# Block-product projections beside attention: sums in place, first output weights in four buffers, and the probabilities turned one product later

## The chip, the cores and the metric

The kernel runs on one core of one Trainium2 chip. The metric is device time in microseconds (us), the median of three runs. Five engines work side by side, each through its own queue in order: TensorE (PE: matrix products; PEld is its weight load), VectorE (DVE), ScalarE (ACT), GpSimd (POOL) and SyncE (SP, which here only issues DMAs). They wait for one another through semaphores.

## The reference, cut to what matters

Three residual layers act on 512 tokens of width 2048, and a norm ends the program. Everything is float32. The change lies in the third layer:

```python
def odd_layer(x, norm_g, w_in, b_forget, w_out):
    hn = rmsnorm(x, norm_g)
    proj = hn @ w_in
    q, k, v, z, f_logit = jnp.split(proj, cuts, axis=-1)
    log_f = jax.nn.log_sigmoid((f_logit + b_forget).astype(jnp.float32))
    o = forgetting_attention(q.reshape(shp), k.reshape(shp), v.reshape(shp), log_f)
    o = o * jax.nn.silu(z)
    return x + o @ w_out
```

There are 16 heads of width 128. `forgetting_attention` is causal softmax attention whose logits get the difference of two running sums of `log_f`.

## The kernel before

**Split operands.** A float32 operand is held as two parts, a rounded upper part (`_hi`) and the rest (`_lo`), and each product is three matmuls: hi by hi, hi by lo, lo by hi. ScalarE rounds (Copy into `w_hi`, `act_hi`), GpSimd or VectorE subtracts (`w_lo`, `act_lo`). Activations lie transposed, 16 tiles (`kt`) of 128 features by 512 tokens. A weight tile has 128 output columns in two halves of 8 `kt`, each 512 KB. Half 0 comes into `raw[:, 0]`, half 1 into `raw[:, 1]`, and `w_hi`, `w_lo` have four slots. `cast` (line 761) rounds a half; `rest` (line 3341) on GpSimd subtracts it in two instructions of 128x512 and raises `split_done`.

**Into the third layer (the forget stage).** `norm_vector(2)` scales each of 16 tiles into one of four buffers `norm_in` (line 721), ScalarE rounds it (706), VectorE subtracts (728). `first_tensor` multiplies the tiles of the forget logits and of head 0's q, then come k, v and the gate of head 0 as plain products (`gemm`, lines 338 to 340), 48 matmuls each. `first_vector` (441, 444) finishes the first two outputs, and ScalarE evacuates them (2679, 2682). TensorE's product for v waits for the evacuation of q. `forget_vector` and `forget_scalar` work out the running sum of the forget gates (16 rows) and store it as `decays`.

**The block products (w7).** The heads 1 to 15 have their projections made while attention for the head before runs. A pair of 128-column tiles by all tokens is done with 7 instead of 8 half-size products (Strassen, in Winograd's form). Each product is 24 matmuls of 128x256 (lines 2036 to 2039). The activation sides are S1 to S4, sums of quarters of the normed activations. They are made once, in two parts q = 0, 1 of four `kt` each. Before the change `fold_whole` (line 1897) first adds `act_hi` and `act_lo` back together into buffers of `arena`, four instructions for each q. `fold_sums` (1903 to 1909) makes the four sums and the rest of S1 (1911), `fold_round` (1919) rounds S1, S2, S4 on ScalarE, and `fold_gpsimd` (1926) subtracts S2 and S4. The two q share buffers, so q = 1 waits for GpSimd's rest of q = 0. S3 goes over a part of `act_hi` and `act_lo` (1934, 1939) once the gate's product has read it. `w7_vector` makes the weight sides in place (T1 2103, T2 2107, T3 2109, T4 2113; rests 2119), `w7_cast` (2053) rounds, and `w7_gpsimd` (2130) subtracts five of the seven. The raw quarters "11", "12", "21", "22" come from SyncE (`fetch`, 1978).

**One unit** is attention of head u and two w7 pairs (0 and 1) for head u+1. TensorE's order in `unit` is: scores (2177, `s`), product 0 of pair 0, the turn of v (2154), products 1 to 3, transposes of the probabilities (2188, `tp`), products 4 to 6, probabilities by v (2196, `pv`), the seven products of pair 1. The transposes wait for VectorE's scaling of the probabilities (2352, `sc3`), and `pv` waits for the lower part of the turned probabilities (2356, `pl`), which follows ScalarE's rounding (2231, `pt`). Product 4 needs `x2`, product 2's evacuation (2069), which stands behind the exponentials (2226) in ScalarE's queue. There are 15 such units, and a last attention without w7 pairs.

**Out of attention.** The last attention has the third output projection's first two tiles beside it (`gemm_two`, 362 to 364). It starts when three halves of their weights are split. Their four halves come through the two `raw` buffers in order: half 0 and half 1 of the first tile, then of the second, each load waiting for GpSimd to be done with the half before it in that buffer. The heads' results, stored in `mixed`, are loaded back into `mix` in five parts (line 3320), 3.75 MB.

## Time and profile before

| what | value |
|---|---|
| median of 3 runs | 3012.54 us (3011.49 to 3013.39) |
| the profiled execution | 3011.28 us, its span 3009.4 us |
| TensorE busy | 2894.2 us, 96% of the span |
| VectorE, ScalarE, GpSimd busy | 1594.5, 1302.0, 1432.3 us |
| mean granted TensorE clock | 0.99 |

Each execution's own time is 1.9 us over its span. A busy TensorE leaves only its waits to win, as its instructions stay the same here; so the profile is read for where TensorE sits idle, for how long, and what it waits for. The trace puts each wait down to the instruction that ended it. The stages are found by line: 338 to 340 plain products, 2036 to 2039 block products, 362 to 364 the first two output tiles.

### The profile page before, as it was taken

What the parts mean: (1) busy time and instruction counts of PE and PEld (TensorE: products, weight loads), DVE (VectorE), ACT (ScalarE), POOL (GpSimd) and SP (SyncE); (2) the same over time, 40 slices, a digit from 0 to 9 for tenths busy, and PEclk for the clock granted to TensorE, in tenths of its full rate; (3) what the DMA queues carried; (4) which work ended last, traced back from release to release, by engine and by line L of the source; (5) the groups of instructions that cost most, each with busy time, mean ns of one, the idle gap of its engine ahead of it and who ended that gap; (6) DMA issues with size and microseconds to landing.
All of it is one profiled execution on the core that took longest, in us unless ns stands there. A gap on an engine that the chain in (4) does not pass through costs nothing.

```text
span 3009.4 us, 52820 instructions
## 1 busy us (share of the span) xinstructions
PE 2894.2 (96%) x20478; PEld 2433.6 (81%) x20478; DVE 1594.5 (53%) x2101; ACT 1302.0 (43%) x1777; POOL 1432.3 (48%) x1037
## 2 busy tenths in 40 slices
PE   8999999999999999999999999996999999999898
PEld 6777777777877887887787778875999999999787
DVE  7555565343444138777723352146777767777312
ACT  6433344255655233333335453234455454545422
POOL 1223332533245446666543334434666666666643
PEclk9999999999999999999999999998999999999999
DMA  5111111222123433222242234431223222222433
GB/s 216 57 59 58 58 58 58 94 74 82 58 84 109 147 115 112 91 93 92 101 137 91 84 112 133 146 106 64 95 98 103 100 100 102 94 94 98 147 124 117
DMA packets 98561, 298.17 MB, mean 99 GB/s; under 512 B 10608, under 2 KB 16880, under 8 KB 97408
## 3 DMA queue, kind: packets, MB, share of 16 engines
q1 hardware_dynamic: 71440, 246.12, 24.2%
q10 hardware_dynamic: 26992, 50.22, 4.9%
q8 instruction: 95, 1.56, 0.2%
q14 instruction: 34, 0.28, 0.0%
HBM read 273.45 MB, written 22.84 MB: 98 GB/s over the span
## 4 chain that ended last, share of the span: by engine, by line
PE 77%; DVE 10%; issue 6%; ACT 3%; POOL 2%; DMA 1%; DVEq 0%; ACTq 0%; POOLq 0%; SPq 0%
PE ps L338 8%; PE ps L340 8%; PE ps L339 8%; PE ps L2036 6%; PE ps L2039 6%; PE ps L2038 6%; PE ps L1028 4%; PE ps L1029 4%; PE ps L1030 4%; PE ps L1348 3%; PE ps L1350 2%; PE ps L1349 2%; POOL w_lo L3341 2%; DVE arena L3147 1%; PE ps L1413 1%
## 5 line engine op out<-in xcount | busy, mean ns | idle before, releaser
L3341 POOL TENSOR_TENSOR w_lo<-raw,w_hi 128x512 fp32r<-128x512 f32 x632 | 849.6, 1368 | 1243.4 <-ACT w_hi L761 1242.3
L338 PE MATMUL ps<-act_hi,w_hi 128*128 128x512 f32 x1232 | 485.9, 394 | 17.5 <-POOL w_lo L3341 12.5
L761 ACT ACTIVATE w_hi<-raw 128x1024 fp32r<-128x1024 f32 x320 | 337.4, 1055 | 361.9 <-PE ps L340 142.8
L340 PE MATMUL ps<-act_lo,w_hi 128*128 128x512 f32 x1232 | 480.4, 390 | 0.0
L339 PE MATMUL ps<-act_hi,w_lo 128*128 128x512 f32 x1232 | 480.1, 390 | 0.0
L2130 POOL TENSOR_TENSOR w_lo<-raw,w_hi 128x512 fp32r<-128x512 f32 x150 | 233.8, 1579 | 151.1 <-ACT w_hi L2053 151.1
L338 PEld LDWEIGHTS ps<-act_hi,w_hi 128*128 128x128 f32 x1232 | 231.6, 188 | 78.9 <-issue 22.7
L1028 PE MATMUL ps<-act_hi,w_hi 128*128 128x512 f32 x736 | 294.5, 400 | 0.0
L1029 PE MATMUL ps<-act_hi,w_lo 128*128 128x512 f32 x736 | 287.1, 390 | 0.0
L1030 PE MATMUL ps<-act_lo,w_hi 128*128 128x512 f32 x736 | 286.9, 390 | 0.0
L2130 POOL TENSOR_TENSOR w_lo<-arena,w_hi 128x512 fp32r<-128x512 f32 x150 | 223.5, 1510 | 121.0 <-ACT w_hi L2053 120.2
L2036 PE MATMUL ps<-act_hi,w_hi 128*128 128x256 f32 x960 | 274.7, 286 | 0.0
L2039 PE MATMUL ps<-act_lo,w_hi 128*128 128x256 f32 x960 | 272.9, 284 | 0.0
L2038 PE MATMUL ps<-act_hi,w_lo 128*128 128x256 f32 x960 | 272.7, 284 | 0.0
L340 PEld LDWEIGHTS ps<-act_lo,w_hi 128*128 128x128 f32 x1232 | 231.6, 188 | 48.9
L339 PEld LDWEIGHTS ps<-act_hi,w_lo 128*128 128x128 f32 x1232 | 231.8, 188 | 47.6 <-issue 0.7
L531 DVE TENSOR_TENSOR mix<-ps,arena 128x512 f32 (+1 forms) x46 | 31.7, 692 | 394.3 <-PE ps L340 370.1
L2036 PEld LDWEIGHTS ps<-act_hi,w_hi 128*128 128x128 f32 x960 | 185.6, 193 | 0.8
L2038 PEld LDWEIGHTS ps<-act_hi,w_lo 128*128 128x128 f32 x960 | 185.3, 193 | 0.8
L2039 PEld LDWEIGHTS ps<-act_lo,w_hi 128*128 128x128 f32 x960 | 185.2, 193 | 0.0
L1348 PE MATMUL ps<-act_hi,w_hi 128*128 128x512 f32 x384 | 168.7, 439 | 0.0
L1028 PEld LDWEIGHTS ps<-act_hi,w_hi 128*128 128x128 f32 x736 | 138.4, 188 | 34.3 <-issue 5.5
(492 smaller groups left out, 5979.9 us busy)
## 6 DMA issues: line engine op xcount, KB each, us to landing
raw<-stream SPq DMA_DIRECT2D x380, 512.0 KB, 3.3
arena<-stream SPq DMA_DIRECT2D x62, 512.0 KB, 3.3
residual<-mix ACTq DMA_DIRECT2D x32, 256.0 KB, 2.0
arena<-residual ACTq DMA_DIRECT2D x32, 256.0 KB, 2.7
arena<-x_rows SPq DMA_DIRECT2D x4, 1024.0 KB, 18.2
arena<-x ACTq DMA_DIRECT2D x16, 256.0 KB, 2.7
kept_qk<-mix ACTq DMA_DIRECT2D x16, 256.0 KB, 2.0
arena<-kept_qk ACTq DMA_DIRECT2D x16, 256.0 KB, 3.6
```

The lines of the kernel that those rows point to most:

```text
L338: pe.matmul(dst, w_hi[:, slot, j, :], act_hi[:, a, :], start=first, stop=False)
L339: pe.matmul(dst, w_lo[:, slot, j, :], act_hi[:, a, :], start=False, stop=False)
L340: mm = pe.matmul(dst, w_hi[:, slot, j, :], act_lo[:, a, :], start=False, stop=last)
L761: nc.scalar.activation(w_hi[:, s, :, :], src[:, s % 2, :, :], ACT.Copy).then_inc(cast_done, 1)
L1028: self.pe.matmul(dst, w_hi[:, slot, j, :], act_hi[:, kt, :], start=kt == 0, stop=False)
L1029: self.pe.matmul(dst, w_lo[:, slot, j, :], act_hi[:, kt, :], start=False, stop=False)
L1030: mm = self.pe.matmul(dst, w_hi[:, slot, j, :], act_lo[:, kt, :], start=False, stop=kt == KT - 1)
L2036: pe.matmul(dst, w_hi[:, slot, j, :], hi[:, j, :], start=first and j == 0, stop=False, skip_group_check=True)
L2038: pe.matmul(dst, w_lo[:, slot, j, :], hi[:, j, :], start=False, stop=False, skip_group_check=True)
L2039: mm = pe.matmul(dst, w_hi[:, slot, j, :], lo[:, j, :], start=False, stop=j == HK - 1, skip_group_check=True)
L2130: last = nc.gpsimd.tensor_tensor(w_lo[:, slot, part, :], w7_buffer(pp, W7_SOURCE[i])[:, part, :], w_hi[:, slot, part, :].bitcast(F32), ALU ...
L3341: last = nc.gpsimd.tensor_tensor(w_lo[:, s, part, :], raw[:, s % 2, part, :], w_hi[:, s, part, :].bitcast(F32), ALU.subtract)
```

## The change

Three edits, and their helpers:

1. **Sums in place.** In norm 2 the scaled tile overwrites its tile of `mix`, where it stays whole, so `fold_whole` goes (8 instructions of VectorE). The four sums of each q are made in place in `mix`. S1 and S3 of q = 0 are made at the end of `norm_vector`, S2 and S4 of q = 0 at the start of `forget_vector`, those of q = 1 in one row while ScalarE does the logarithm. Their upper parts go to free slots of `arena` and, for S3 and S4, over parts of `act_hi` and `act_lo`, and the rests go in place in `mix`. The rounding of S3 and S4 waits for the gate's half 0. ScalarE takes k's evacuation and the gate's weights before the forget gate's exponential. SyncE no longer waits for `decays` and q before the first fetches. VectorE splits q and k of head 0 ahead of T1, l1 and the rest of S3.
2. **Probabilities turned one product later.** `fill(0, 1, 2, 3, 4)` stands ahead of the transposes in place of `fill(0, 1, 2, 3)`, and `fill(0, 5, 6)` behind.
3. **First output weights in four buffers.** The four halves go to the four buffers of the w7 quarters (`OUT3_RAW`). ScalarE rounds them in the order 2, 0, 3, 1 between its rounding of the results, and GpSimd subtracts in that order. The first 8 results come into `arena` instead of `mix`. Numbers of later loads and casts are shifted (`elsewhere`).

```diff
@@ norm_scalar, norm_vector (norm_in[j] stays for norm 1)
+                nc.scalar.activation(act_hi[:, ft, :], norm_in[i % 4] if norm == 1 else mix_tile(ft),
...
+            if norm == 2:
+                dve.wait_ge(norm_lo, KT * (norm + 1))
+                fold_sums(dve, 0, "13")
             first_vector(dve, (0, N_U, N_F)[norm], norm)
@@ the sums
+        s_raw = {"1": half_k(mix_k[:, high_k, :], 1), "2": half_k(mix_k[:, low_k, :], 0),
+                 "3": half_k(mix_k[:, low_k, :], 1), "4": half_k(mix_k[:, high_k, :], 0)}
+        s_hi = {"1": eight(arena_r, 26), "2": eight(arena_r, 18), "3": half_k(act_hi[:, low_k, :], 1),
+                "4": half_k(act_lo[:, low_k, :], 1)}
...
+        def fold_sums(dve, q, names):
+            x11, x21, x22, x12 = (four(s_raw[n], q) for n in "2314")
+            F, tt = fold_sum, nc.vector.tensor_tensor
+            for name in names:
+                if name == "1":
+                    F.mark(tt(x22, x21, x22, ALU.add), f"s1{q}")
+                elif name == "3":
+                    F.wait(dve, f"s1{q}", 0)
+                    F.mark(tt(x21, x11, x21, ALU.subtract), f"s3{q}")
...
+        def fold_round(act, name, q):
+            if name in "34":
+                act.wait_ge(pe_half, 2 * (N_ODD + 3) + 1)
+            fold_sum.wait(act, f"s{name}{q}", 0)
+            fold_act.mark(nc.scalar.activation(four(s_hi[name], q), four(s_raw[name], q), ACT.Copy), f"h{name}{q}")
@@ w7_sync
             sp.wait_ge(split_done, 2 * N_OUT3)
-            sp.wait_ge(decay_stored, 16)
-            sp.wait_ge(evac_act, N_ODD + 1 - ODD_SHIFT)
@@ the first output weights
+        OUT3_RAW = [w7_raw[r] for r in (0, 2, 1, 3)]
+        OUT3_ORDER = (2, 0, 3, 1)
+        def out3_sync(sp, load_to):
+            last = W7_PAIRS - 1
+            w7_prep.wait(sp, "T3", last)
+            sp.wait_ge(w7_lo, 5 * last + 2)
+            load_to(OUT3_RAW[0], N_OUT3, 0).then_inc(out3_loaded[0], 16)
+            sp.wait_ge(mixed_stored, 16 * W7_UNITS)
+            for part, product, first in ((0, 1, 26), (1, 1, 28), (2, 2, 18)):
+                f0, f1 = MIX_PARTS[part]
+                sp.wait_ge(w7_pe, 7 * last + product + 1)
+                sp.dma_start(slots(arena, first, f1 - f0).rearrange("p (a t) -> p a t", t=T),
+                             mixed[f0:f1, :, :].rearrange("a p t -> p a t")).then_inc(mix_loaded[part], 16)
+                if part == 1:
+                    sp.wait_ge(w7_lo, 5 * last + 3)
+                    load_to(OUT3_RAW[1], N_OUT3, 1).then_inc(out3_loaded[1], 16)
+            sp.wait_ge(w7_lo, 5 * last + 5)
+            load_to(OUT3_RAW[2], N_OUT3 + 1, 0).then_inc(out3_loaded[2], 16)
+            load_to(OUT3_RAW[3], N_OUT3 + 1, 1).then_inc(out3_loaded[3], 16)
+            for part in (3, 4):
...
+        def out3_cast(act, i):
+            act.wait_ge(out3_loaded[i], 16)
+            act.wait_ge(w7_pe, 7 * W7_PAIRS - (1, 0, 3, 2)[i])
+            nc.scalar.activation(w_hi[:, i, :, :], OUT3_RAW[i], ACT.Copy).then_inc(out3_hi[i], 1)
@@ w7_gpsimd
+                        if first_pair(u, pp) and i == 0:
+                            fold_gpsimd(pool, "4")
@@ attention_tensor, unit
-                fill(0, 1, 2, 3)
+                fill(0, 1, 2, 3, 4)
                 early(0, 8)
                 V.wait(pe, "sc3", u)
...
-                fill(0, 4, 5, 6)
+                fill(0, 5, 6)
@@ attention_scalar, head
+            evacuated(act, N_ODD + 2, lambda: nc.scalar.activation(at_v_in, ps[:, N_ODD % 2, :], ACT.Copy))
             w7_cast(act, 0, 0, 0, 0)
...
+            for name in "43":
+                for q in range(2):
+                    fold_round(act, name, q)
             w7_cast(act, 0, 0, 0, 1)
@@ attention_vector, head
-            prepare(0, 0, 0, "T1")
-            prepare(0, 0, 0, "l1")
-            fold_last_rest(dve)
-            fold_pool.wait(dve, "l41", 0)
             tt(at_q_lo, at_q_in, at_q.bitcast(F32), ALU.subtract).then_inc(at_first, 1)
...
+            prepare(0, 0, 0, "T1")
+            prepare(0, 0, 0, "l1")
+            fold_vector(dve, "3", 0)
+            fold_vector(dve, "3", 1)
```

**Place 1, the forget stage, ScalarE.** From the evacuation of q (first row) to the rounding of the gate's first half of weights, before:

```order
L2682 ACTIVATE arena<-arena 128x512
L2684 ACT_TABLE_LOAD
L2684 ACTIVATE arena<-arena 16x512
L2686 ACT_TABLE_LOAD
L2686 ACTIVATE arena<-arena,eps 16x512
L2688 DMA decays<-arena 16x512
L1919 ACTIVATE mix_r<-arena 128x1024 x2
L1919 ACTIVATE arena_r<-arena 128x1024
L761 ACTIVATE w_hi<-raw 128x1024
```

The same stretch now:

```order
L2734 ACTIVATE arena<-arena 128x512
L1915 ACTIVATE arena_r<-mix 128x1024 x2
L765 ACTIVATE w_hi<-raw 128x1024
L2738 ACTIVATE arena<-ps 128x512
L765 ACTIVATE w_hi<-raw 128x1024
L2740 ACT_TABLE_LOAD
L2740 ACTIVATE arena<-arena 16x512
```

The gate's weights (761, now 765) moved from behind the forget gate's chain and three roundings to behind two roundings.

**Place 1, VectorE.** From the end of the sums to the last row that the first scores wait for (2416, now 2464), before:

```order
L1911 TENSOR_TENSOR mix_r<-arena,mix_r 128x1024
L2406 CAST arena_r<-arena 128x512
L2103 TENSOR_TENSOR raw<-arena,raw 128x1024
L2119 TENSOR_TENSOR w_lo<-raw,w_hi 128x1024
L1939 TENSOR_TENSOR act_lo<-arena,act_hi 128x4x256 x2
L2412 TENSOR_TENSOR arena_r<-arena,arena_r 128x512
L2414 CAST arena_r<-arena 128x512
L2416 TENSOR_TENSOR arena_r<-arena,arena_r 128x512
```

and now:

```order
L1922 TENSOR_TENSOR mix_r<-mix,arena_r 128x4x256 x2
L2458 CAST arena_r<-arena 128x512
L2460 TENSOR_TENSOR arena_r<-arena,arena_r 128x512
L2462 CAST arena_r<-arena 128x512
L2464 TENSOR_TENSOR arena_r<-arena,arena_r 128x512
L2147 TENSOR_TENSOR raw<-arena,raw 128x1024
L2163 TENSOR_TENSOR w_lo<-raw,w_hi 128x1024
L1922 TENSOR_TENSOR mix_r<-mix,act_hi 128x4x256 x2
```

The splits of q and k went ahead of the weight sum T1, its rest l1 and the rest of S3, which are now between the first scores' operands and the second weight sum.

**Place 2, out of attention, ScalarE.** From the last rounding of a w7 weight (first row) to the turn's copy of v (2220, now 2266), before:

```order
L2053 ACTIVATE w_hi<-arena 128x1024
L2273 ACT_TABLE_LOAD
L2273 ACTIVATE arena<-arena 128x512
L670 ACTIVATE act_hi<-mix 128x512 x8
L2072 ACTIVATE arena<-ps 128x256
L761 ACTIVATE w_hi<-raw 128x1024 x4
L2220 ACTIVATE arena_r<-ps 128x512
```

and now:

```order
L2097 ACTIVATE w_hi<-arena 128x1024
L2023 ACTIVATE w_hi<-raw 128x1024
L2321 ACT_TABLE_LOAD
L2321 ACTIVATE arena<-arena 128x512
L2038 ACTIVATE act_hi<-arena 128x512 x4
L2023 ACTIVATE w_hi<-raw 128x1024
L2023 ACTIVATE w_hi<-arena 128x1024
L2038 ACTIVATE act_hi<-arena 128x512 x4
L2116 ACTIVATE arena<-ps 128x256
L2023 ACTIVATE w_hi<-arena 128x1024
L2266 ACTIVATE arena_r<-ps 128x512
```

Three of the four weight roundings moved ahead of the last evacuation `c21` (2072, now 2116), on which the turn of the last head's v waits.

## Rows read from the trace of the kernel before

**Rows 1.** Waits of TensorE, whole program: us in total, times, longest.

```profile
PE ps L2188 <- DVE arena L2352: 27.5, 15, 2.1
PE ps L2177 <- DVE arena_r L2416: 17.5, 1, 17.5
PE ps L362 <- issue: 9.6, 1, 9.6
```

**Rows 2.** Timeline of TensorE, forget stage: start, us, instruction, [idle before <-releaser].

```profile
2028.16 0.47 PE L338 MATMUL ps<-act_hi,w_hi 128*128 128x512 f32 x1 [0.89 <-issue]
...
2047.51 0.76 PE L338 MATMUL ps<-act_hi,w_hi 128*128 128x512 f32 x1 [8.18 <-POOL w_lo L3341]
...
2077.72 3.89 PE L2177 MATMUL ps<-arena_r 128*128 128x128 f32 x12 [17.52 <-DVE arena_r L2416]
2081.41 0.34 PE L2036 MATMUL ps<-act_hi,w_hi 128*128 128x256 f32 x1
```

**Rows 3.** Busy time and granted clock (third number from the right) in a stretch.

```profile
2061.00:2077.00 16.00, 0.00 (x0) 0.00 (x0) 10.12 (x10) 7.96 (x9) 8.35 (x4) 0.61 0.05 16
```

**Rows 4.** Timeline, the other engines in the forget stage.

```profile
2019.96 1.47 DVE L728 TENSOR_TENSOR act_lo<-arena,act_hi 128x512 fp32r<-128x512 f32 x2
2023.87 1.29 DVE L441 TENSOR_TENSOR arena<-ps,arena 128x512 f32<-128x512 f32 x2 [2.44 <-ACT arena L709]
...
2042.76 1.04 ACT L761 ACTIVATE w_hi<-raw 128x1024 fp32r<-128x1024 f32 x1
...
2021.73 5.06 POOL L3341 TENSOR_TENSOR w_lo<-raw,w_hi 128x512 fp32r<-128x512 f32 x4 [2.90 <-ACT w_hi L761]
```

**Rows 5.** Source line 1897, 2043 to 2051: durations in ns, min/median/max.

```profile
L1897 DVE TENSOR_TENSOR arena<-act_hi,act_lo x3: 1217/2279/2290, 2042.8 to 2046.2; 128x1024 f32<-128x1024 f32 x3
```

**Rows 6.** Timeline of TensorE, one unit of the loop.

```profile
2367.31 0.34 PE L2177 MATMUL ps<-arena_r 128*128 128x128 f32 x2
2369.23 0.27 PE L2036 MATMUL ps<-act_hi,w_hi 128*128 128x256 f32 x1
...
2381.18 0.28 PE L2039 MATMUL ps<-arena_r,w_hi 128*128 128x256 f32 x1
...
2383.36 1.31 PE L2188 MATMUL ps<-ident,arena 128*128 128x128 f32 x10 [1.90 <-DVE arena L2352]
2384.43 0.36 PE L2036 MATMUL ps<-act_hi,w_hi 128*128 128x256 f32 x1
...
2393.14 0.63 PE L2196 MATMUL ps<-arena_r 128*128 128x512 f32 x2
```

**Rows 7.** Timeline of the other engines in that unit.

```profile
2380.28 0.39 ACT L2069 ACTIVATE w_x<-ps 128x256 f32<-128x256 f32 x1
2380.64 2.66 DVE L2352 TENSOR_SCALAR arena<-arena,at_st 128x128 f32<-128x128 f32 x4
...
2384.71 1.24 ACT L2231 ACTIVATE arena_r<-ps 128x1280 fp32r<-128x1280 f32 x1 [2.14 <-PE ps L2188]
2387.93 1.48 DVE L2356 TENSOR_TENSOR arena_r<-ps,arena_r 128x1280 fp32r<-128x1280 f32 x1
```

**Rows 8.** Timeline, end of the w7 pairs and first output weights.

```profile
2812.09 0.77 PE L362 MATMUL ps<-act_hi,w_hi 128*128 128x512 f32 x1 [9.61 <-issue]
...
2795.39 4.26 ACT L670 ACTIVATE act_hi<-mix 128x512 fp32r<-128x512 f32 x8
...
2808.36 1.06 ACT L761 ACTIVATE w_hi<-raw 128x1024 fp32r<-128x1024 f32 x1 [5.62 <-DMA raw<-stream]
...
2790.89 2.55 POOL L2130 TENSOR_TENSOR w_lo<-arena,w_hi 128x512 fp32r<-128x512 f32 x2
```

**Rows 9.** DMA issues, 2784 to 2800: KB each, median us to landing.

```profile
raw<-stream SPq DMA_DIRECT2D x2, 512.0 KB, 7.0
```

**Rows 10.** The page's section 6, the same loads over the whole program.

```profile
raw<-stream SPq DMA_DIRECT2D x380, 512.0 KB, 3.3
```

**Rows 11.** Timeline of ScalarE, out of attention: a table load.

```profile
2789.98 1.28 ACT L2273 ACT_TABLE_LOAD   x1
```

More of the change, by code:

```diff
@@ L733, in norm_vector @@
                     rest(i - 2)
-                if i >= 4:
+                if norm == 1 and i >= 4:
                     dve.wait_ge(norm_lo, KT * norm + i - 3)
@@ L1883, in part_of @@
-        def part_of(view, q, second_k, second_t):
-            k0 = HK * second_k + 4 * q
-            return view[:, k0:k0 + 4, HT * second_t:HT * second_t + HT]
-        def fold_whole(dve, q):
-            t = fold_t[q]
-            if q == 0:
-                fold_dve.start(0)
-            for name, k, half in (("x11", 0, 0), ("x21", 0, 1), ("x22", 1, 1), ("x12", 1, 0)):
-                if q and name == "x22":
-                    fold_dve.wait(dve, "l10", 0)
-                if q and name == "x12":
-                    fold_pool.wait(dve, "l40", 0)
-                fold_dve.mark(nc.vector.tensor_tensor(t[name], part_of(act_hi, q, k, half).bitcast(F32),
-                                                      part_of(act_lo, q, k, half).bitcast(F32), ALU.add), f"{name}{q}")
@@ new lines, in build_program, with four @@
+        fold_act = Steps(sem("fold_act"), "h10 h20 h11 h21 h40 h41 h30 h31")
+        fold_dve = Steps(sem("fold_dve"), "l10 l11 l30 l31")
+        fold_pool = Steps(sem("fold_pool"), "l20 l21 l40 l41")
+        for steps in (fold_sum, fold_act, fold_dve, fold_pool):
+            steps.start(0)
+        def four(view, q):
+            return view[:, 4 * q:4 * q + 4, :]
+        def fold_sums(dve, q, names):
[7 more added lines that the diff above has]
+                    F.mark(tt(x21, x11, x21, ALU.subtract), f"s3{q}")
+                elif name == "2":
+                    F.wait(dve, f"s3{q}", 0)
+                    F.mark(tt(x11, x22, x11, ALU.subtract), f"s2{q}")
+                else:
+                    F.wait(dve, f"s2{q}", 0)
+                    F.mark(tt(x12, x12, x11, ALU.subtract), f"s4{q}")
@@ new lines, in out3_round, with out3_rest @@
+        def out3_round(act, tiles):
+            for ft in tiles:
+                nc.scalar.activation(act_hi[:, ft, :], slots(arena, 26 + ft if ft < 4 else 14 + ft),
+                                     ACT.Copy).then_inc(mix_hi, 1)
+        def out3_rest(dve):
+            for ft in range(HK):
+                dve.wait_ge(mix_hi, KT * 2 + ft + 1)
+                nc.vector.tensor_tensor(act_lo[:, ft, :], slots(arena, 26 + ft if ft < 4 else 14 + ft),
+                                        act_hi[:, ft, :].bitcast(F32), ALU.subtract).then_inc(mix_early, 1)
@@ L2670, in build_program @@
         fg = Steps(sem("fg"), "y mn n e l ls cum")
-        fg_t = [slots(arena, 18 + j)[0:FR, :] for j in range(4)]
+        fg_t = [slots(arena, 7 + j)[0:FR, :] for j in range(4)]
         def forget_tensor(pe):
@@ L3334, in _, with rest @@
             last.then_inc(eps_set, 1)
[L3336 to L3338 removed]
+            def rest(m, s, elsewhere=0):
+                pool.wait_ge(cast_done, m + (1 - elsewhere))
                 for k0 in (0, HK // 2):
@@ L3343, in rest, with rests @@
                 last.then_inc(split_done, 1)
-            def rests(m0, m1):
+            def rests(m0, m1, elsewhere=0):
                 for m in range(m0, min(m1, -(-m0 // 4) * 4)):
-                    rest(m, m % 4)
+                    rest(m, m % 4, elsewhere)
                 if -(-m0 // 4) < m1 // 4:
```

169 lines of the change are left out of this document (72 added, 97 removed).

## The prediction

> **What bounds the kernel now.** I read the waits of TensorE first. It is busy for 96% of the span and the change leaves its instructions alone, so time comes only from its idle stretches and from its clock. Three of its longest waits belong to this change [rows 1]: 27.5 us in 15 pieces ahead of the transposes, 17.5 us once ahead of the first scores, 9.6 us once ahead of the first output tiles; and a fourth of 8.2 us for the gate's weights [rows 2]. That is 62.8 us, an upper bound without the clock. Then the timeline of TensorE shows where each stands [rows 2, 6, 8], the timelines of the others what was late, and the granted clock what the idle time costs afterwards.
>
> **Part A, transposes after product 4.** In a unit of the loop the last matmul of product 3 starts at 2381.18 and the transposes at 2383.36, 1.90 us idle [rows 6]. Products 4 to 6 start at 2384.43 and `pv` at 2393.14, 72 matmuls later, so they start 0.12 us apart, and a product takes 2.9 us; the transposes could have started at 2381.30. The unit loses 2.06 us. Product 4 goes into that place and the transposes come 2.9 us later, at 2384.2.
>
> Are their operands there? The scaling that they wait for runs from 2380.64 to 2383.30 [rows 7], so 0.9 us are left over. Is product 4 ready at 2381.30? It waits for `x2`, whose evacuation ends at 2380.67 [rows 7]: 0.6 us over. What is late next is `pv`. It had three products of cover behind the transposes and now has two, 5.8 us. Its chain is the rounding `pt` of 1.24 us right behind the transposes (1.3 us after 2384.2, so 2385.5 to 2386.8), then the subtraction `pl` of 1.48 us, to 2388.3 [rows 7]. Before, that subtraction started at 2387.93 since VectorE stood at the sum that waits for product 4, which now comes earlier. `pv` starts at 2393.14 before [rows 6], about 2391.1 now, so 2.8 us are left over. The rest of VectorE's queue (T1 to l2 of pair 1) comes some 0.9 us later against TensorE than before, beside slack of 3 us and more. So the wait goes, and nothing takes its place at first sight. Fifteen units: 27.5 us by the waits, 27.5 + 15 x 0.16 = 29.9 us by the starts. As the two margins of 0.6 and 0.9 us are thin and VectorE's instructions stretch beside GpSimd's (below), I take **28 us**, with ends of 20 and 30.
>
> **Part B, the forget stage.** The gate's product starts at 2047.51, 8.18 us after v's product, because its weights were rounded only at 2042.76 [rows 2, 4], behind the forget gate's chain and three roundings in ScalarE's queue. Now two roundings of 1.06 us stand ahead; I place the first weight rounding at some 2034 and GpSimd's half, 2.5 us, at some 2037, ahead of 2041 when TensorE asks. That wait goes. The first scores waited another 17.52 us, up to 2077.72, for VectorE, which had done eight additions of `act_hi` and `act_lo`, eight sums, and had waited for shared buffers in between. The eight additions (1.22 us each, 2.28 when GpSimd runs [rows 5]) and that wait are gone.
>
> The new line of TensorE: v's product starts at 2028.16 and its 48 matmuls take 11.2 us to the end of the last one at 2039.33 (8.18 us before 2047.51) [rows 2]; the gate's takes as long, and one follows the other 0.16 us before its modelled end, so both are 22.1 us. From scores to product 0 are 1.92 us at full clock [rows 6]. 2028.16 + 22.1 + 1.9 gives product 0 at 2052.2 in place of 2081.41: 29.2 us. That holds 25.7 us of waits and 3.5 us of clock: in the idle stretch before the scores the granted clock is 0.61 [rows 3], and the twelve score matmuls then take 3.89 us [rows 2], twice their time, so they run at the lower of the two levels (1.2 GHz); the rest of the 3.5 us lies in the gate's product, which also comes out of an idle stretch.
>
> Two things go off that. First, S1 and S3 of q = 0 now stand between the last rest of the norm (ends 2021.43) and `first_vector` (starts 2023.87, after 2.44 us idle) [rows 4]. Two sums take 2.45 us alone, so they would fit exactly; but GpSimd is busy from 2021.73 for 5.06 us [rows 4], and a 128x1024 sum beside it takes 2.28 instead of 1.22 us [rows 5]. That is 0 to 2.1 us later for `first_vector`, for q's evacuation, and so for v's product, which waits for it (0.89 us idle now). I take 2.1, as both run at once. Second, unit 0. With v's product at 2030.3 the scores are due at 2052.4. VectorE must by then have ended four sums of q = 1 (from some 2035), the scan, two rests of S1, and the two splits; GpSimd works beside it all the time. I get 2045 without stretching, and 2052.5 with 1.06 us more for each of seven instructions, so 0 to 0.5 us of wait there. Behind it come T1, l1 (whose rounding waits for four roundings of S4 and S3, which wait for the gate's half 0 at some 2047), two rests of S3, T2, the scores' decay, T3, l2: product 2 is due at 2060.9 and l2 comes at 2061 to 2065. A wait of 0.5 to 4.5 us; I take 3. So B is 29.2 - 2.1 - 3.1 = **24 us**, with ends of 18 (all stretched and another chain late) and 29.
>
> On the stretching the Trainium skill has a rule (SBUF — State Buffer, section "Who interferes with whom"): a VectorE instruction with two inputs in SBUF shares a port with GpSimd's reads, and the one that comes second waits for the whole of the other's instruction. The trace shows 1.06 us more, less than a whole GpSimd instruction of 1.26 us (5.06 / 4). By the rule at its hardest, with every one of the nine instructions behind a whole GpSimd one, B would be 1.8 us less.
>
> **Part C, out of attention.** `gemm_two` starts at 2812.09 after 9.61 us idle; the third of its four halves was rounded at 2808.36 after 5.62 us waiting for its load [rows 8], which had waited for a buffer. Now the first half in use (number 2) is loaded when GpSimd is done with pair 29, at 2793.44 [rows 8]. Loads take 7.0 us in this stretch [rows 9], since 3.75 MB of results are being fetched, but of these 1.75 MB stand behind it now; I put its landing at 2797.5 (bounds 2796.8 with the 3.3 us of the whole program [rows 10], and 2800.5 with 7.0). ScalarE then stands in line: this rounding 1.06, table load 1.28 [rows 11], silu 0.6, four roundings 2.1 (eight take 4.26 [rows 8]), number 0 and number 3 another 2.1, so 2804.6; GpSimd's rests of 0 and 3 follow, 5.1 us from the end of number 0's rounding at 2803.6 on, to 2808.9. The turn of v waits for `c21`, behind four more roundings, at 2807.1, and hides. So `gemm_two` starts at some 2809.5: **2.5 us**, with ends of -1 (late landing: the wait only changes its name, from a load to `c21` and the rests) and 5, where a shorter cold stretch is counted too.
>
> **Sum.** 28 + 24 + 2.5 = 54.5 us. On the profiled execution, 3011.3 us, that is 2956.8; the median is 1.2 us higher, so **2958 us**. All the rest of the program is the same instructions in the same order.
>
> **Rivals.** (1) *The loop keeps a good part.* The 0.6 us that `x2` has over rests on exponentials behind a table load, and the 0.9 us of the scaling on VectorE instructions that GpSimd stretches in part of the units (2.66 us for the four scalings). If contention shifts by one GpSimd instruction a unit, 1 us comes back in each: 15 us, giving 2973. For it speaks how thin the margins are; against it, that fourteen units wait the same 1.9 to 2.1 us. (2) *The forget stage is bound elsewhere*: load, T1, rounding, l1, l2 of the first pair are one chain through three engines that runs in a crowded stretch. If it makes unit 0 wait 10 us in place of 3, with some cold matmuls behind it, 2966 to 2968. (3) *Slower than before: `pv` becomes the wait.* It has two products of cover in place of three, 5.8 us, and its chain is 3.1 us after the transposes. From 5.8 us on TensorE waits; to lose all 54.5 us it must wait 3.6 us in each of 15 units, so the point that decides is a chain of 9.4 us, three times the rows'. That needs VectorE or ScalarE to queue something long between, which their order doesn't show. At 11 us it gives 15 x 1.6 = 24 us over break-even, 3036. (4) *The change does nothing in C*: `c21` and the third rest are as late as the load was; 2960.5, inside the forecast's range.
>
> **How the numbers follow.** Forecast 0.68 (with rival 4), rival 1 0.15, rival 2 0.11, rival 3 0.03, about no change 0.02 (losses in all three parts), something faster than the ends 0.01. The range from the ends of the parts is 3012.5 - 64 = 2948 at best and 3012.5 - 37 = 2975 at worst; for both rivals together I put **2946 to 2978**. A measurement of this kernel tells 0.2%, 6 us, from no change: faster 0.95, same 0.02, slower 0.03.
>
> **What would show it.** Right: no wait of TensorE at the transposes above 0.3 us, units 2 us shorter than now; v's and the gate's products back to back, the scores near 2052 and at full clock; a wait of a few us at product 2 of unit 0 on l2; `gemm_two` 1 to 4 us earlier against the end of the pairs, its wait now on GpSimd's third rest. Wrong: a wait at product 4 for ScalarE's `x2` or at `pv` for VectorE's subtraction in each unit; a start of v's product beyond 2031; an idle stretch of over 5 us in unit 0.

## The result

The changed kernel takes **2979.62 us** (median of 4 runs, 2978.01 to 2981.58) against 3012.01 us for the kernel before on the same chip (3011.31 to 3013.39): ratio 0.9892, 95% interval 0.9875 to 0.9909. The profiled execution has a span of 2977.4 us against 3009.4. So 32 us were gained where 54.5 were forecast: the time fell, as forecast, but it lies 21.6 us above the forecast and 1.6 us above the upper end of the range. I compare the starts of the scores of unit 1, S(1), of the last attention, S(15), and of `gemm_two`:

| | before | after | gained up to here | forecast |
|---|---|---|---|---|
| S(1) | 2126.07 | 2111.96 | 14.1 | 25.9 |
| S(15) | 2799.95 | 2769.55 | 30.4 (loop: 16.3) | 52.0 (loop: 26.1) |
| `gemm_two` | 2812.09 | 2780.20 | 31.9 (here: 1.5) | 54.5 (here: 2.5) |

The forecast column is my own working cut at these places: part B's 24 us and one of part A's fifteen units up to S(1), fourteen units in the loop, part C behind.

### The profile page after: what moved, and what is told of

It reads as the page before. It is cut to its first block, busy times and chain, and to the rows that moved or that the text cites. A ratio compares the mean times of both kernels' runs of the same rounds, so it can differ in the third digit from the quotient of the medians.

```text
span 2977.4 us, 52806 instructions
## 1 busy us (share of the span) xinstructions
PE 2895.6 (97%) x20478; PEld 2434.5 (82%) x20478; DVE 1646.9 (55%) x2093; ACT 1303.8 (44%) x1777; POOL 1445.8 (49%) x1037
## 4 chain that ended last, share of the span: by engine, by line
PE 57%; POOL 15%; issue 14%; DVE 10%; ACT 1%; DMA 1%; DVEq 0%; POOLq 0%; ACTq 0%; SPq 0%
POOL w_lo L2174 13%; PE ps L338 8%; PE ps L340 8%; PE ps L339 8%; PE ps L1032 4%; PE ps L1034 4%; PE ps L1033 4%; PE ps L1352 3%; PE ps L1354 2%; PE ps L1353 2%; DVE arena L3200 1%; POOL w_lo L3386 1%; PE ps L1417 1%; PE ps L1084 1%; DVE arena L3230 1%
## 5 line engine op out<-in xcount | busy, mean ns | idle before, releaser
L338 PEld LDWEIGHTS ps<-act_hi,w_hi 128*128 128x128 f32 x1232 | 232.0, 188 | 71.5 <-issue 15.2
L2174 POOL TENSOR_TENSOR w_lo<-arena,w_hi 128x512 fp32r<-128x512 f32 x150 | 231.3, 1562 | 110.7 <-ACT w_hi L2097 110.4
L2083 PE MATMUL ps<-mix_r,w_hi 128*128 128x256 f32 x960 | 272.2, 283 | 0.0
L340 PEld LDWEIGHTS ps<-act_lo,w_hi 128*128 128x128 f32 x1232 | 232.0, 188 | 49.0
L2083 PE MATMUL ps<-act_lo,w_hi 128*128 128x256 f32 x720 | 204.0, 283 | 0.0
L2080 PEld LDWEIGHTS ps<-act_hi,w_hi 128*128 128x128 f32 x960 | 184.4, 192 | 0.8
L2083 PEld LDWEIGHTS ps<-mix_r,w_hi 128*128 128x128 f32 x960 | 184.9, 193 | 0.0
```

Of the source, the lines that this page charges most:

```text
L338: pe.matmul(dst, w_hi[:, slot, j, :], act_hi[:, a, :], start=first, stop=False)
L340: mm = pe.matmul(dst, w_hi[:, slot, j, :], act_lo[:, a, :], start=False, stop=last)
L2080: pe.matmul(dst, w_hi[:, slot, j, :], hi[:, j, :], start=first and j == 0, stop=False, skip_group_check=True)
L2083: mm = pe.matmul(dst, w_hi[:, slot, j, :], lo[:, j, :], start=False, stop=j == HK - 1, skip_group_check=True)
L2174: last = nc.gpsimd.tensor_tensor(w_lo[:, slot, part, :], w7_buffer(pp, W7_SOURCE[i])[:, part, :], w_hi[:, slot, part, :].bitcast(F32), ALU ...
```

## The profile after

Waits of TensorE, whole program, the rows that answer to [rows 1] (us in total, times, longest):

```profile
PE ps L2080 <- DVE w_lo L2163: 15.7, 14, 4.7
...
PE ps L2200 <- ACT arena L2116: 6.0, 1, 6.0
PE ps L2223 <- DVE arena_r L2464: 5.0, 1, 5.0
...
PE ps L2234 <- DVE arena L2404: 2.2, 2, 1.1
```

The waits at the transposes (2234, before 2188) are down from 27.5 to 2.2 us. A new line stands on top: product 2 of pair 0 (2080) waits for VectorE's rest `l2` (2163), 4.7 us in unit 0 and 0.8 to 0.9 in each of 13 others. The scores (2223) wait 5.0 us in place of 17.5, and out of attention the turn of v (2200) waits 6.0 us for `c21` (2116), and `gemm_two` another 1.5, in place of 9.6. With the waits for the plain products' weights (12.5 us before, 4.3 after) TensorE waits 32.4 us less by these rows, about what the time fell by.

**The forget stage.** Timeline of TensorE, answering to [rows 2] (start, us, instruction, idle before and its releaser):

```profile
2028.43 0.47 PE L338 MATMUL ps<-act_hi,w_hi 128*128 128x512 f32 x1 [1.85 <-issue]
...
2057.10 3.89 PE L2223 MATMUL ps<-arena_r 128*128 128x128 f32 x12 [5.05 <-DVE arena_r L2464]
...
2072.84 0.39 PE L2080 MATMUL ps<-arena_r,w_hi 128*128 128x256 f32 x1 [4.67 <-DVE w_lo L2163]
```

The product for v starts at 2028.43, and the gate's follows with no wait, as forecast. But v's product takes 12.6 us where 11.2 were forecast, so the two end at 2052.05, 23.6 us after v's start and not 22.1. The rows show it in the granted clock (third number from the right) at the start of v's product, behind a wait of 1.85 us: here, and in the same stretch of the later run e2, where the product took 11.0 us.

```profile
2028.40:2032.00 3.60, 3.57 (x10) 2.83 (x11) 2.50 (x3) 2.19 (x3) 0.00 (x0) 0.59 0.50 164
```

```profile
2029.40:2033.00 3.60, 3.59 (x16) 2.97 (x17) 1.87 (x2) 1.51 (x2) 0.00 (x0) 1.00 0.46 162
```

Nothing ahead of this place differs between the two kernels, so it is a matter of the single execution (of the eleven profiles with this stage eight are like the first, three like the second). And since VectorE sets the start of the scores in both, it only makes the wait before them shorter (5.05 us here, 7.28 in e2). Then come two waits, 5.05 us before the scores, which again run at the lower clock (3.89 us), and 4.67 before product 2. The other engines in between:

```profile
2042.38 2.88 DVE L2761 TENSOR_TENSOR arena<-arena 16x512 f32<-16x512 f32 x1
2045.29 3.30 DVE L2763 TENSOR_TENSOR_SCAN arena<-arena 16x512 f32<-16x512 f32 x1
...
2054.33 2.71 DVE L2464 TENSOR_TENSOR arena_r<-arena,arena_r 128x512 fp32r<-128x512 f32 x1
2056.97 3.39 DVE L2147 TENSOR_TENSOR raw<-arena,raw 128x1024 f32<-128x1024 f32 x1
...
2041.33 6.19 POOL L1922 TENSOR_TENSOR mix_r<-mix,arena_r 128x1024 fp32r<-128x1024 f32 x2
2050.66 3.36 POOL L2174 TENSOR_TENSOR w_lo<-raw,w_hi 128x512 fp32r<-128x512 f32 x2 [3.14 <-ACT w_hi L2097]
2053.98 5.29 POOL L1922 TENSOR_TENSOR mix_r<-mix,act_lo 128x1024 fp32r<-128x1024 f32 x2
```

VectorE's 16-row sum and scan, the last split of k and T1 each lie at least in part beside a GpSimd subtraction of 128x1024 (rests of S2, then of S4). The rows show how the stretching works: the scan ends 1.07 us after the subtraction beside it (2048.59 and 2047.52), T1 1.09 us after its own (2060.36 and 2059.27), about as long as either takes alone (1.2 us). So they begin in earnest only when GpSimd's instruction is over.

**One unit of the loop.** A unit takes (2769.55 - 2111.96) / 14 = 46.97 us, before 48.13. TensorE has one wait in it:

```profile
2347.22 2.08 PE L2223 MATMUL ps<-arena_r 128*128 128x128 f32 x12
...
2356.30 0.38 PE L2080 MATMUL ps<-arena_r,w_hi 128*128 128x256 f32 x1 [0.84 <-DVE w_lo L2163]
```

VectorE and GpSimd in that unit: T1, the decay, T3 (2153), `l2` (2163), and the rests of the weights 3 and 4.

```profile
2344.46 1.23 DVE L2147 TENSOR_TENSOR raw<-arena,raw 128x1024 f32<-128x1024 f32 x1 [2.37 <-POOL w_lo L2174]
...
2349.44 1.69 DVE L2383 TENSOR_TENSOR ps<-ps,arena 128x128 f32<-128x128 f32 x4
...
2351.77 2.17 DVE L2153 TENSOR_TENSOR arena<-arena 128x1024 f32<-128x1024 f32 x1
2353.86 2.31 DVE L2163 TENSOR_TENSOR w_lo<-raw,w_hi 128x1024 fp32r<-128x1024 f32 x1
...
2351.57 7.01 POOL L2174 TENSOR_TENSOR w_lo<-arena,w_hi 128x512 fp32r<-128x512 f32 x4 [7.24 <-ACT w_hi L2097]
```

The same instructions of the kernel before, in the unit of [rows 6] (T3 is line 2109 there, `l2` line 2119), and product 2:

```profile
2371.86 1.22 DVE L2109 TENSOR_TENSOR arena<-arena 128x1024 f32<-128x1024 f32 x1
2373.00 2.32 DVE L2119 TENSOR_TENSOR w_lo<-raw,w_hi 128x1024 fp32r<-128x1024 f32 x1
...
2370.70 7.03 POOL L2130 TENSOR_TENSOR w_lo<-arena,w_hi 128x512 fp32r<-128x512 f32 x4 [7.24 <-ACT w_hi L2053]
...
2375.45 0.38 PE L2036 MATMUL ps<-mix_r,w_hi 128*128 128x256 f32 x1
```

Before, `l2` ended at 2375.32, and product 2 started at 2375.45: there was no margin at all, 0.13 us. After, GpSimd's rests start 4.35 us after the scores' start in place of 3.39, and T3, at +4.55 in both kernels, now takes 2.17 us instead of 1.22. GpSimd's first subtraction of 128x512 takes 1.3 us: before, it ended at +4.68, 0.13 us after T3's start; now it ends at +5.64, and T3 is done 1.08 us after that. T3 is slow over the whole program (groups by line, of before and of after; busy, mean ns of one):

```profile
L2109 DVE TENSOR_TENSOR arena<-arena 128x1024 f32<-128x1024 f32 x15 | 20.8, 1384 | 0.0
```

```profile
L2153 DVE TENSOR_TENSOR arena<-arena 128x1024 f32<-128x1024 f32 x15 | 32.5, 2165 | 0.0
```

And T1 waits longer for GpSimd's last rest of the pair before (waits of VectorE, before and after):

```profile
DVE raw L2103 <- POOL w_lo L2130: 19.3, 14, 1.4
```

```profile
DVE raw L2147 <- POOL w_lo L2174: 32.6, 14, 2.4
```

**Out of attention**, answering to [rows 8]:

```profile
2777.61 1.08 PE L2200 MATMUL ps<-ident,arena 128*128 128x128 f32 x4 [5.98 <-ACT arena L2116]
2780.20 0.77 PE L362 MATMUL ps<-act_hi,w_hi 128*128 128x512 f32 x1 [1.50 <-issue]
...
2768.14 1.06 ACT L2023 ACTIVATE w_hi<-raw 128x1024 fp32r<-128x1024 f32 x1 [8.58 <-DMA raw<-stream]
...
2777.10 0.36 ACT L2116 ACTIVATE arena<-ps 128x256 f32<-128x256 f32 x1
```

## The experiments

Each was timed beside the kernel before, which took 3011.22 to 3011.92 us.

### The loop

My theory for the loop's missing 10 us is a **ring** through four engines. In TensorE's queue the transposes now stand one product behind product 2. From them the chain goes on by ScalarE's `pt`, VectorE's `pl`, T1, `l1` and T2 of pair 1, ScalarE's roundings, GpSimd's five rests of pair 1, VectorE's T1 and T2 of the next pair 0, ScalarE's rounding, T3 and `l2`, and back to product 2. Moving the transposes later moves all of it later against TensorE, and the slack at its end was 0.13 us. The rival is that the wait comes from elsewhere in the change.

**e1: the turn alone.** The kernel before with edit 2 only:

```diff
-                fill(0, 1, 2, 3)
+                fill(0, 1, 2, 3, 4)
...
-                fill(0, 4, 5, 6)
+                fill(0, 5, 6)
```

> The kernel before with the second edit alone: product 4 ahead of the transposes. Theory R (a ring closes): with the transposes a product later, VectorE's T1 and T2 of pair 1, then GpSimd's five rests, then T1 and T2 of the next unit come about 0.9 us later against TensorE; ScalarE's rounding 3 and GpSimd's rest 3 follow and collide with VectorE's T3, so l2 is 0.9 us late and product 2 waits. It needs nothing of the other two edits, so the unit is 46.85 us here too (47.96 before) and the whole gains 16 to 17 us: 2995 us. Rival (the wait for l2 comes from the other edits or from how the first unit starts): the unit is 45.9 us, 28 us gained, 2984 us.

Measured: 2996.09 us, ratio 0.9948 (0.9931 to 0.9965). Its waits of TensorE have the line that the whole change has:

```profile
PE ps L2036 <- DVE w_lo L2119: 11.2, 13, 0.9
```

Edit 2 alone gives 15.4 us, not 28, and makes the new wait by itself.

**e11: the turn undone in the changed kernel** (the same diff, backwards).

> The changed kernel with edit 2 undone: the transposes stand ahead of product 4 again. Edit 2 alone (e1) gave 15.4 us. If the parts add up, 2979.6 + 15.4 = 2995 us, with TensorE waiting 1.9 us at the transposes of each of 15 units. If instead the forget stage's parts and the turn lean on each other (unit 0 then waits for its scaling rather than for l2, and gains nothing of the turn), 2992 to 2993 us.

Measured: 2997.01 us, ratio 0.9953 (0.9938 to 0.9968), with the old wait back, `PE ps L2234 <- DVE arena L2404: 27.1, 15, 2.1`. Seen from this side edit 2 is worth 17.4 us and the rest of the change 14.9. With e1's 15.4 the parts make 30.3 of 32.4 us. The executions of e11 lie up to 4.9 us apart, so as far as can be told the parts add up.

**e2: `l2` ahead of the decay.** The changed kernel with VectorE's queue in a unit rewritten, so that the ring's last two steps no longer stand behind the decay:

```diff
                 prepare(u, par, 0, "T2")
-                decayed(u)
                 prepare(u, par, 0, "T3")
                 prepare(u, par, 0, "l2")
+                decayed(u)
                 largest(u)
-                prepare(u, par, 0, "T4")
                 scaled(u)
                 w7_sum_out(dve, u, 0, "c12")
+                prepare(u, par, 0, "T4")
```

> The changed kernel, in each unit VectorE makes T3 and l2 of pair 0 ahead of the decay of the scores, and T4 behind c12. Theory R: l2 is there 2.4 us or more before product 2, its wait (0.83 to 0.93 us a unit) goes, the units are 45.9 us and TensorE bound: 13 us faster than the changed kernel, about 2966 us. Rival (VectorE's whole queue between scores and scaling is the bound, so that any order gives the same): the wait moves to the transposes, 2979 us.

Measured: 2962.87 us, ratio 0.984 (0.9823 to 0.9856), 16.8 us less than the changed kernel. No wait at product 2 or at the transposes is left in the loop, and a unit is 45.9 us, what part A had promised (48.13 less 2.06):

```profile
2339.25 2.08 PE L2223 MATMUL ps<-arena_r 128*128 128x128 f32 x12
...
2385.19 1.03 PE L2223 MATMUL ps<-arena_r 128*128 128x128 f32 x7
```

**e3: T4 alone moved.** The same edit without the move of `decayed`: T4 goes behind the scaling and `c12`, T3 and `l2` stay where they are.

> The changed kernel with T4 of pair 0 behind the scaling and c12, T3 and l2 left where they are. Theory R: the scaling ends up to 2 us earlier, nobody waits for it, product 2's wait for l2 stays at 0.9 us: the time stays at 2979 us within 2. Rival (the scaling and VectorE's whole queue bind): faster by 5 to 13 us.

Measured: 2998.9 us, ratio 0.9962 (0.9948 to 0.9976), 19 us slower than the changed kernel: a miss. The trace shows why. ScalarE's rounding behind T4 and GpSimd's rests behind that come later, so T1 of pair 1 now waits as well (timeline of VectorE; then waits of VectorE and of TensorE):

```profile
2377.94 1.23 DVE L2147 TENSOR_TENSOR arena<-arena 128x1024 f32<-128x1024 f32 x1 [1.16 <-POOL w_lo L2174]
```

```profile
DVE raw L2147 <- POOL w_lo L2174: 50.3, 14, 3.7
...
DVE arena L2147 <- POOL w_lo L2174: 17.5, 15, 1.2
```

```profile
PE ps L2080 <- DVE w_lo L2163: 34.8, 15, 5.9
```

The ring has a second way in, through GpSimd, which I hadn't counted. What is added there arrives at product 2: its wait grows by 19.1 us, from 15.7 to 34.8. By the starts the units are 48.04 us in place of 46.97, which is 15.0 us from S(1) to S(15); the rest of the loss lies ahead of S(1) and behind S(15), 1.0 and 1.7 us, and in the difference between executions. It also says that e2's gain is the move of the decay, as T4 moves in both. e2 has T4 as late, and T1 starts there even 1.4 us later against the scores than in the changed kernel (2337.89 to 2339.25, beside 2344.46 to 2347.22), but with the decay behind it `l2` ends 6.0 us after the scores' start instead of 8.9.

**e4: half of GpSimd's rests of pair 1 left out.**

```diff
-                        for k0 in (0, HK // 2):
+                        for k0 in ((0, HK // 2) if pp == 0 else (0,)):
```

> Leaves out work: GpSimd subtracts only the first half (128x512) of each of the five weights of pair 1, in pair 0 all of them. Theory R: T1 of the next unit comes some 7 us earlier, T2 no longer ends after the scores, GpSimd's rest 3 starts some 0.9 us earlier and T3 (2.17 us in the changed kernel, 1.3 before) no longer waits behind it; product 2's wait goes, units of 45.9 us, 14 us; and at the end of the pairs GpSimd is done some 6 us earlier, which brings the first output weights 4 us forward: about 2961 us. Rival (T3 and l2 are late only because GpSimd's rests of pair 0, untouched here, run beside them): the wait of 0.9 us stays, the time falls by the 4 us at the end only, 2975 us.

Measured: 2961.93 us, ratio 0.9836 (0.9819 to 0.9852). VectorE's wait in T1 falls, and TensorE's at product 2 is left in unit 0 alone:

```profile
DVE raw L2147 <- POOL w_lo L2174: 7.0, 14, 0.5
```

```profile
PE ps L2080 <- DVE w_lo L2163: 5.8, 1, 5.8
```

Shortening the ring on GpSimd, without touching VectorE's order, gives what e2 gives. The total met the expectation, its parts didn't: a unit is 45.62 us (0.28 less than in e2), so the loop gave 18.9 us and not 14, and `gemm_two` starts only 1.3 us earlier against S(15), not 4. T3 didn't become short either, it takes 1.63 to 1.88 us. But GpSimd's rests start 2.6 to 2.8 us after the scores, `l2` then takes 1.21 us instead of 2.3, and it ends 7.3 to 7.6 us after the scores' start, where product 2 is due at 8.1. With e1 to e3 and e11 that settles the loop.

### The forget stage

**e5: GpSimd's rests of S2 behind its first weight's rest.**

```diff
-            fold_gpsimd(pool, "2")
             w7_gpsimd(pool)
...
                         if first_pair(u, pp) and i == 0:
+                            fold_gpsimd(pool, "2")
                             fold_gpsimd(pool, "4")
```

> The changed kernel, GpSimd's rests of S2 (two of 128x1024, 6.19 us from 2041.33) moved behind its first weight of pair 0, with those of S4. Theory: VectorE's sum of the forget gate (2.88 us for 16 rows) and scan (3.30) were stretched by them; alone they take 0.7 and 1.2 us, so the store of the decays, ScalarE's first rounding of a w7 weight and the split of q and k come some 4 us earlier, the first scores wait 1 us at most in place of 5.0, and product 2 of the first unit 3 to 5 us (4.7 now): 3 to 5 us faster, 2975 to 2977. Rival (the gate sum and the scan are slow for another reason, or the chain load, T1, l1, l2 isn't moved by it): no change, 2979.6.

Measured: 2979.08 us, ratio 0.9892 (0.9875 to 0.9908), no gain: a miss. The small instructions did become short, and the scores came 3.7 us earlier (2053.38, 0.84 us waited), but products 1 (1.20 us of wait) and 2 gave it back (VectorE, then TensorE, then GpSimd):

```profile
2042.88 0.67 DVE L2762 TENSOR_TENSOR arena<-arena 16x512 f32<-16x512 f32 x1
2043.58 1.21 DVE L2764 TENSOR_TENSOR_SCAN arena<-arena 16x512 f32<-16x512 f32 x1
...
2053.25 3.41 DVE L2147 TENSOR_TENSOR raw<-arena,raw 128x1024 f32<-128x1024 f32 x1
...
2059.93 4.54 DVE L1922 TENSOR_TENSOR mix_r<-mix,act_hi 128x1024 fp32r<-128x1024 f32 x2
...
2072.33 0.58 PE L2080 MATMUL ps<-arena_r,w_hi 128*128 128x256 f32 x1 [9.14 <-DVE w_lo L2163]
...
2055.53 6.72 POOL L1922 TENSOR_TENSOR mix_r<-mix,act_lo 128x1024 fp32r<-128x1024 f32 x2
```

The stretching moved from the sum and the scan to the first rest of S3 (4.54 us for the two, 2.35 in the changed kernel) and to `l1` (2.22 instead of 1.22), which stand on the same path to `l2`. Product 2 starts 1.0 us earlier against v's product than in the changed kernel, and this goes again in colder matmuls behind the longer wait: the granted clock from 2072 to 2078 is 0.52, against 0.66 from 2073 to 2078 there.

**e6: VectorE's rests of S1 behind the splits of q and k**, ahead of T1 (two lines moved).

> The changed kernel, VectorE's two rests of S1 moved from ahead of the split of q and k to behind it (ahead of T1). Theory (l2 of the first pair is what binds the first unit; the wait at the scores is only part of the way to it): the scores start 2 us earlier, product 2 waits 2 us longer, no change of the time, 2979.6 within 1. Rival (the two waits are independent): 2 us faster.

Measured: 2979.55 us, ratio 0.9891 (0.9875 to 0.9908), as expected no change: 1.31 us of wait before product 0, 3.15 before product 1 and 6.94 before product 2 replace 5.05 and 4.67. The scores start at 2053.17, 3.9 us earlier and not the 2 expected, and all of it comes back. Both runs say that the stage ends with VectorE's `l2`, and that neither of these two changes of order ahead of it matters.

**e10: GpSimd's rests of S2 and S4 cut to a quarter.** e2 with

```diff
-                   (s_hi["2"], s_lo["2"]),
-                   (s_hi["4"], s_lo["4"]),
+                   (s_hi["2"], s_hi["2"]),
+                   (s_hi["4"], s_hi["4"]),
...
-            fold_rest(pool, fold_pool, nc.gpsimd.tensor_tensor, name, q)
+            fold_rest(pool, fold_pool, nc.gpsimd.tensor_tensor, name, q, 1)
```

> e2 (l2 ahead of the decay), and GpSimd's four rests of S2 and S4 cut to a quarter of their elements; the block products take the upper parts of S2 and S4 in place of their rests, so the output is not the reference's. Theory (in the forget stage VectorE's small instructions and the weight sum T1 are stretched by GpSimd's long subtractions): the 16-row sum takes 0.67 instead of 2.88 us, the scan 1.2 instead of 3.3, the splits 0.7 each instead of up to 2.7, the scores start at 2053 to 2054 instead of 2058.74 and nearer to full clock; product 2 waits up to 2.5 us, as T1's rounding stands behind four roundings of S4 and S3 on ScalarE; 4 to 6 us less than e2, 2957 to 2959 us. Rival (the stage is bound by the chain of load, T1, rounding, l1, T2, T3, l2 whatever GpSimd does): the wait only moves from the scores to product 2 as it did in e5, 2962 us or more.

Measured: 2956.51 us, ratio 0.9817 (0.9802 to 0.9832), 6.4 us less than e2.

```profile
2051.84 2.18 PE L2223 MATMUL ps<-arena_r 128*128 128x128 f32 x12 [1.37 <-DVE arena_r L2464]
...
2062.20 0.38 PE L2080 MATMUL ps<-arena_r,w_hi 128*128 128x256 f32 x1 [1.95 <-DVE w_lo L2163]
...
2042.46 1.22 DVE L2761 TENSOR_TENSOR arena<-arena 16x512 f32<-16x512 f32 x1
...
2051.71 1.76 DVE L2147 TENSOR_TENSOR raw<-arena,raw 128x1024 f32<-128x1024 f32 x1
```

The scores start at 2051.84 and run near full clock (2.18 us), product 2 waits 1.95 us, and S(1) is at 2101.53, 24.5 us ahead of the kernel before. As executions differ by up to 2 us in when v's product starts, I compare from there to S(1): 97.9 us before, 83.5 in the changed kernel, 80.1 in e2, 73.1 here. So of the stage's length `l2` behind the decay costs 3.4 us (with it ahead, T3 and `l2` also take 1.22 us each and not 2.22 and 2.29), and the four long subtractions cost 7.0. That is what the rows make of the stretching: from e2 to e10 the 16-row sum goes from 2.88 to 1.22 us, the scan from 3.29 to 1.65, the last split from 2.71 to 0.69 and T1 from 3.38 to 1.76, 6.9 us together. The wait out of attention grew by 1.0 us (6.9 to 7.9), which leaves the 6.4 of the medians, roughly.

### Out of attention, and the versions that gain

**e7: `gemm_two` starts at two split halves.**

```diff
-                    pe.wait_ge(split_done, n * 2 + h + 3)
+                    pe.wait_ge(split_done, n * 2 + h + (2 if layer == 2 and h == 0 else 3))
```

> The changed kernel, but the first output tiles start when two halves of their weights are split (the two that they read first) in place of three. Theory: the third half's rest, stretched beside VectorE's rests of the results, holds the start at 2780.2; with two the turn of v and its wait for c21 hold it, until 2778.7: 1.5 us faster, 2978.1. Rival (c21 holds it anyway): no change.

Measured: 2978.97 us, ratio 0.989 (0.9874 to 0.9907). Its `gemm_two` starts 2.1 us earlier against S(15) (8.57 in place of 10.65), but its matmuls then take 13.6 instead of 12.6 us; 0.65 us less than the changed kernel can't be told from none.

**e8: combined.** e2, e5 and e7 together; ScalarE rounds the output weights in the order 0, 2, 3, 1, and does `c21` right behind `silu` in place of behind eight roundings of results.

> The changed kernel with VectorE's order of the second run (T3 and l2 of pair 0 ahead of the decay, T4 behind c12), GpSimd's rests of S2 late, and out of attention: start at two halves, halves rounded in the order 0, 2, 3, 1, c21 right behind the silu. Theory: 17 us from the loop, 3 to 5 from the forget stage, 5 to 6 out of attention (the start bound by the load of half 2, then c21 and the first rounded results, at 2774 in the changed kernel's time): 2954 us, faster than both. Rival (the gains hide one another): 2960 or more.

Measured: 2960.59 us, ratio 0.9831 (0.9815 to 0.9847): 2.3 us less than e2, the rival's figure. `gemm_two` starts 5.1 us after S(15) in place of 10.65, but a new wait stands at the last transposes:

```profile
2772.84 1.54 PE L2235 MATMUL ps<-ident,arena 128*128 128x128 f32 x6 [5.95 <-DVE arena L2406]
```

VectorE takes the last attention's decay only at 2764.30, behind its eight rests of results, though the scores are done at 2752.7.

**e9: the decay first.** e8 and

```diff
-            out3_rest(dve)
             decayed(u)
             largest(u)
+            out3_rest(dve)
```

> The combined kernel e8, and in the last attention VectorE's decay, diagonal and maxima stand ahead of the eight rests of the results instead of behind them. Theory (the gain out of attention was hidden by VectorE's queue: in e8 it is idle from 2748.4 to 2754.88 while the scores are done by 2752.7, then spends 2.5 + 6.5 us on the rests and only then takes the decay, and TensorE waits 5.95 us at the transposes): decay to maxima lie at 2752.8 to 2756.9, the rests behind them, gemm_two starts 1 to 2 us later than in e8, and the scaling ends some 3 to 5 us earlier; TensorE's wait at the transposes falls to under 1.5 us, scores to the end of gemm_two 39.35 -> 36 us, 2957 us. Rival (TensorE must wait for the same sum of VectorE's work either way, and the wait only moves from the transposes to the start of gemm_two and into its matmuls): 2960 us or more.

Measured: **2957.36 us**, ratio 0.982 (0.9806 to 0.9833), 54.6 us less than the kernel before and 22.3 less than the changed one.

```profile
2758.18 0.75 PE L362 MATMUL ps<-act_hi,w_hi 128*128 128x512 f32 x1 [2.94 <-DVE act_lo L2045]
...
2771.09 1.31 PE L2235 MATMUL ps<-ident,arena 128*128 128x128 f32 x10 [0.15 <-DVE arena L2406]
```

From S(15) to the first plain product behind attention are 35.1 us, against 39.7 in e8, 39.9 in e2 and 38.2 in the changed kernel. So part C's place held 3 us more. The step that gave them is VectorE's order, in which alone e9 differs from e8; whether earlier loads would give more wasn't tried.

## Why the prediction was right or wrong

**What bounds: right.** All that was gained came out of the three waits and the one for the gate's weights, and TensorE's instructions stayed as they were. Of my own signs, the units were only 1.2 us shorter and not 2, and of the signs of being wrong one came: an idle stretch of over 5 us in unit 0, by a hair (5.05).

**Part A: the step that failed is "beside slack of 3 us and more".** The wait at the transposes went (27.5 to 2.2 us). I had worked out the margins of `x2`, of the scaling and of `pv`, and these held: no wait at product 4 or at `pv`. But I put the rest of VectorE's queue at 0.9 us later with slack in plenty, and didn't lay `l2` beside product 2. It had 0.13 us. The 0.96 us by which GpSimd's rests came later (3.39 to 4.35) fell on T3 and returned as 0.84 us of wait in each unit. The loop gave 16.3 of 26.1 us; e2 shows that the forecast's 45.9 us a unit was there to be had. Rival 1 named the size and the right family (a late instruction of VectorE beside GpSimd), but at the scaling; its chance of 0.15 was far too low for margins that I had called thin.

**Part B: the term "less 3.1 us" was mis-sized.** The gate's wait went, as forecast. The 29.2 us stand by e10: product 0 starts there 27.9 us earlier against v's product than before, with 1.4 us of wait left ahead of the scores. Of the 2.1 us taken off for S1 and S3 ahead of `first_vector`, 1.0 came (one of the two sums was stretched, to 2.20 us, the other took 1.23), and this execution stood 0.7 us earlier there than the one before. The scores were to start at full clock. They didn't, since VectorE was 5 us late. I had stretched seven instructions by 1.06 us, the figure of [rows 5], where GpSimd runs 128x512 subtractions. Beside the 128x1024 ones of S2 and S4, the 16-row sum went from 0.67 to 2.88 us and the scan from 1.21 to 3.30 (e5 has the short ones), T1 from 1.2 to 3.39, the last split from 0.69 to 2.71. That is 2.0 to 2.2 us each. Ahead of the scores stand the first two and the last split, and five more were stretched by 1.0 to 1.1 us: three sums of q = 1, the split of q and a cast. That makes 11.3 us in eight instructions where I had 7.4 in seven, and the difference, 3.9 us, is most of the 4.6 between my 2052.5 and the scores' start at 2057.10. T1 comes behind the scores' operands, and its 2.2 us fell on product 2, with 1.0 us each of T3 and `l2`: from T1's start to the end of `l2` are 15.8 us, where I had put 8.5 to 12.5. Hence the wait of 4.67 us there. So 9.7 us of waits stand where I took 3.1, and the clock fell. e10 gives the size back: with these subtractions cut to a quarter, and with `l2` first, S(1) comes 24.5 us earlier, of 25.9 forecast.

The rule of the Trainium skill (SBUF — State Buffer, section "Who interferes with whom"), by which the second of two is blocked until the other's instruction is over, was the better guide here than my row of 1.06 us, and the traces agree with it: the stretched instructions end 1.1 us (a scan, or 128x1024) or 0.55 us (the 16-row sum, a split of 128x512) after GpSimd's. What a VectorE instruction loses is what is left of GpSimd's when its turn comes. I had applied the rule with the 1.26 us of a 128x512 subtraction. A 128x1024 one takes 2.5 us where it isn't held up itself, and the stretches beside it are 2.0 to 2.2.

**Part C: nearly right.** 1.5 us of 2.5. The wait changed its name as its lower end had said, from a load to `c21` (5.98 us) and the rests (1.50). What is missing is in two terms: the first load landed 1.4 us ahead of S(15) and not 2.5, and GpSimd's two rests behind it, beside VectorE's, took 5.9 us and not 5.1. The ring has a small share in the first: GpSimd's last rest of the pairs ended 0.9 us later against S(15) than before the change, but where the turn is undone (e11) and it ends as before, the load lands only 0.3 us earlier.

**Rivals.** 1: happened, at another place. 2: it named the chain load, T1, rounding, `l1`, `l2`, and unit 0 with the scores waits 9.7 us where it said 10. Both together (15 + 9 us) were what I had no case for: I weighed them apart, and the range took 2978 as the end for both, though my own two prices add up to 2958 + 15 + 9 = 2982. 3 and 4: didn't happen.

## What to carry to other kernels

When a step of a loop is moved later in one engine's queue, follow what it releases through every engine back to that queue, and write down the slack wherever it is waited for: the tightest place decides, and here it was 0.13 us at a product that the edit didn't name. Where instructions of two engines disturb each other, take the stretch from a row in which the disturbing one has the same length. A wait that goes at one place and comes back whole at the next (e5, e6, e8) says that the bound is the queue behind both, and then its order is what to change (e2, e9).

## What the runs showed of the hardware

- A VectorE instruction that meets a GpSimd subtraction under way ends about its own time after that subtraction does, so its stretch goes with what is left of GpSimd's instruction and not with its own size: a 16x512 sum took 0.67 us alone, 1.22 beside one of 128x256 (e10) and 2.88 beside one of 128x1024; a 16x512 scan 1.21, 1.65 and 3.30. Where the subtraction had 0.13 us left, nothing was added (T3 before the change, 1.22 us).
- Instructions with one input in SBUF were stretched too: a cast of 128x512 took 0.41 us alone and 1.48 beside a 128x512 subtraction (changed kernel, 2052.81). Four scalings of 128x128 to 128x512 (2404) took 1.28 us in e2 with GpSimd all but idle, 2.17 in e3, where the first of them met a subtraction, and 4.48 in the changed kernel's unit. How two queues fall beside each other decides such sums: a shift of 0.96 us in GpSimd's queue made T3 0.95 us longer.
- GpSimd is stretched as well: four subtractions of 128x512 took 5.16 us where VectorE was mostly in PSUM (e2) and 8.61 beside four 128x1024 sums (changed kernel, 2032.77).
- The clock at one and the same place differed between executions: v's product, behind a wait of 1.85 us each time, took 12.6 us with a granted clock of 0.59 in its first 3.6 us (changed kernel), and 11.0 us with 1.00 (e2, e10).
